# NSA layer of a two-block model in fp32: the compressed branch's projection columns first, its chain of steps between the row groups

## The chip, the cores and the metric

One core of a Trainium2 chip runs the whole program in one launch. The metric is the device time of one execution in microseconds (us), as the median of several runs. TensorE is PE in the rows (its weight loads are PEld), VectorE is DVE, ScalarE is ACT, GpSimd is POOL, and SyncE is SP; the SP queue issues the DMA transfers of the weights.

## The reference, cut to what matters

The program computes a first block of two layers, then a second block of two layers, each with a mixer, an output projection and a feed-forward net. The change lies in the mixer of the second block's first layer (NSA). There are 256 tokens, 12 query heads of 64 in 2 groups. With 256 tokens there are only 4 blocks of selectable keys and all are taken, so the selected and the window branch are both causal attention, each with its own keys and values.

```
proj = h @ w_in                       # q | six k/v slices of 128 | 36 gates | 256 memory queries
q = rope(q); k_slc = rope(k_slc); k_win = rope(k_win)
def compress_blocks(u, pos_emb, w1, b1, w2, b2):      # for k_cmp and for v_cmp
    blocks = u[:, idx] + pos_emb[:, None, :]          # 15 overlapping blocks of 32 tokens
    return gelu(flat(blocks) @ w1 + b1) @ w2 + b2     # 2048 -> 256 -> 64
kc = rope(compress_blocks(k_cmp, ...)); vc = compress_blocks(v_cmp, ...)
p_cmp = masked_softmax(q . kc * scale, cmp_end <= t)
gates = sigmoid(gate_logit + gate_b)
o = gates0 * (p_cmp @ vc) + gates1 * o_slc + gates2 * o_win
```

## The kernel before, in words

Every engine runs its own queue in the order in which the code writes it down. There is no scheduler: `nsa_pe`, `nsa_v`, `nsa_a` and `nsa_g` each write the queue of one engine for this stage, and they meet only in semaphores (`put` counts one up, `wait_ge(*got(...))` waits for the count that an event had).

**Weights.** All weights pass through one stream of items, numbered in the order in which PE takes them. An item is at most 1024 columns of 128 partitions. SP loads tiles of at most 2048 columns into three buffers (`raw`) and refills one as soon as the items of the tile three before have been split. ACT copies an item to its rounded part (`split_hi`, L368), DVE subtracts that from the original for the remainder (`split_lo`, L381), and PE multiplies with both, so that each product is made of three passes. There are six places for split items in this stage, so item n can be split only when PE is done with item n-6. ACT and DVE split ahead where the code says so: `split_hi(a, q, event)` splits all items up to the last of that event plus a lead (5 items, 4 for the items of the compression), whatever the item is needed for, and later instructions of the engine wait behind it.

**The NSA stage.** Three groups of rows are projected with tokens on the partitions (`group(0)` and `group(1)`: queries and keys, 4 items each of two chunks x 512 columns; `group(2)`: values and gates, 4 items of 584 columns), and six blocks of 128 columns with features on the partitions (the loop over `c0`, L422 to L427; c0 = 0 and 2 are the compressed keys and values, c0 = 4 the memory queries; an item each). The compression chain is:

- U: 16 small DVE adds (L2363) gather the blocks and add the position term; ACT rounds U (`Uh`, L2507), POOL makes the remainder (`Ul`, L2538);
- steps 0, 1 and 3, 4 (`compress_pe`): two items each of the first compression weight, for keys and for values; ACT copies each result (L2472);
- steps 2 and 5: transposes (L2296), the gelu on ACT (L2479, with a table load), DVE spreads it (`hrep`, L2403);
- step 6: the second weight (L2308, with a DVE add each, L2409); step 7: rope of the compressed keys, a transpose, and the operands `kcB` and `vcB` (L2416 to L2431);
- (b, 0), (b, 1), (b, 2) for both halves b of the tokens: scores (L2326), softmax (DVE L2441 to L2462, ACT L2523), transposes (L2332) and a copy (`cpt`, L2527).

Rope of queries and keys is eight long DVE operations (`rope_v`, L770 to L774). Then `turned_pe` transposes the result (L784) and ACT and DVE copy it out (L803, L798). The gates are an exp on ACT (L2514) and four small DVE operations.

**The attention** runs in rounds of units of two jobs: step 0 is the scores on PE (L619), 1 mask, maximum (DVE L668, L686) and exp (ACT L745), 2 the scaling with 1/sum and gate (DVE L690 to L698, ACT L726), 3 the transposes (PE L628) with copies (ACT L754, DVE L706), 4 the product with the values (PE L643, and the compressed branch's share L646), copied by ACT (L759) and DVE (L720). The list `chain` says which steps of the compression stand ahead of which round. Seven PSUM banks turn in a ring.

## Time and profile before

| what | us |
|---|---|
| median of 3 runs (1324.72 to 1330.0) | 1329.7 |
| profiled execution, its own time | 1329.96 |
| its span on the core | 1328.2 |
| PE busy in it | 1142.6 |
| DVE busy in it | 964.5 |
| ACT busy in it | 692.3 |

The span is what the profiler saw between the first and the last instruction; 1.8 us of the execution's time lie around it. Matmuls overlap, so a busy share of PE is not a share of its peak. The mean granted TensorE clock of the execution is 0.924 of full speed.

### The profile page before, as it was taken

Reading aid. Unit: us, or ns where it says so; the run is one execution under the profiler, and the core shown is the slowest. Engines: PE = TensorE matmul, PEld = TensorE weight load, DVE = VectorE, ACT = ScalarE, POOL = GpSimd, SP = SyncE. Lnnn points to the kernel's source line nnn. Section 1 sums busy time; section 2 is a strip of 40 time slices with the busy share of each in tenths; the row PEclk is TensorE's granted clock in tenths of the full one; section 3 lists DMA queues with packets and bytes.
Section 4 is the critical chain, followed back from the end, with each engine's and each line's share of the span. In section 5 each row is a group of like instructions: output and inputs, shape, how many; then the busy total and the mean of one; then the engine's idle time right before and its main releaser. Section 6 shows DMA issues by size and latency. Waiting matters only on the chain.

```text
span 1328.2 us, 24918 instructions
## 1 busy us (share of the span) xinstructions
PE 1142.6 (86%) x10403; PEld 1062.7 (80%) x10403; DVE 964.5 (73%) x1722; ACT 692.3 (52%) x1261; POOL 151.7 (11%) x113
## 2 busy tenths in 40 slices
PE   6799876979799758948976699999999959999997
PEld 6688765969678748848965599999999848999997
DVE  5787954666778855577768867888867576788873
ACT  5642256555532366555345845565655274565562
POOL 2000000110000001142000001223110000123210
PEclk9999986989899967978986989999999879999999
DMA  8332110344231103415530034554556403455461
GB/s 340 127 100 93 65 64 1 135 151 157 90 128 66 65 1 142 139 69 186 179 128 25 1 129 157 173 177 159 199 203 211 150 1 101 156 173 175 159 207 63
DMA packets 24736, 167.54 MB, mean 126 GB/s; under 512 B 2737, under 2 KB 2865, under 8 KB 8497
## 3 DMA queue, kind: packets, MB, share of 16 engines
q1 hardware_dynamic: 24624, 165.96, 35.8%
q8 instruction: 82, 1.34, 0.4%
q14 instruction: 30, 0.24, 0.1%
HBM read 164.90 MB, written 1.05 MB: 125 GB/s over the span
## 4 chain that ended last, share of the span: by engine, by line
PE 48%; DVE 29%; ACT 17%; issue 4%; DMA 2%; POOL 0%; DVEq 0%; SPq 0%; ACTq 0%; POOLq 0%
PE ps L427 9%; PE ps L422 9%; PE ps L424 9%; DVE WL L381 8%; ACT WH L368 3%; DVE FR L381 3%; PE ps L445 3%; PE ps L453 3%; PE ps L447 3%; ACT ARENA L745 2%; PE ps L643 2%; DMA raw<-wst_in 2%; ACT FR L368 1%; ACT ARENA L2136 1%; ACT L484 1%
## 5 line engine op out<-in xcount | busy, mean ns | idle before, releaser
L381 DVE TENSOR_TENSOR WL<-raw,WH 128x1024 fp32r<-128x1024 f32 (+4 forms) x225 | 274.0, 1240 | 104.6 <-ACT WH L368 104.0
L422 PE MATMUL ps<-FR,WH 128*128 128x256 f32 x1248 | 305.3, 285 | 21.8 <-ACT WH L368 16.5
L424 PE MATMUL ps<-FR,WH 128*128 128x256 f32 x1248 | 301.2, 282 | 1.3 <-DVE FR L493 0.8
L368 ACT ACTIVATE WH<-raw 128x1024 fp32r<-128x1024 f32 (+4 forms) x225 | 218.3, 988 | 101.8 <-PE ps L427 55.4
L422 PEld LDWEIGHTS ps<-FR,WH 128*128 128x128 f32 x1248 | 240.4, 193 | 26.9 <-ACT WH L368 13.6
L424 PEld LDWEIGHTS ps<-FR,WH 128*128 128x128 f32 x1248 | 240.0, 192 | 3.2 <-DVE FR L493 1.9
L422 PE MATMUL ps<-FR,FR 128*128 128x256 f32 x680 | 169.1, 286 | 2.9 <-ACT FR L368 2.2
L427 PE MATMUL ps<-FR,WL 128*128 128x256 f32 x1248 | 170.1, 279 | 0.5 <-DVE WL L381 0.5
L424 PE MATMUL ps<-FR,FR 128*128 128x256 f32 x680 | 167.9, 284 | 0.2 <-DVE FR L493 0.2
L427 PEld LDWEIGHTS ps<-FR,WL 128*128 128x128 f32 x1248 | 155.7, 189 | 0.7 <-DVE WL L381 0.7
L381 DVE TENSOR_TENSOR FR<-raw,FR 128x1024 fp32r<-128x1024 f32 (+2 forms) x100 | 127.3, 1297 | 34.5 <-ACT FR L368 34.5
L422 PEld LDWEIGHTS ps<-FR,FR 128*128 128x128 f32 x680 | 130.4, 192 | 5.4 <-ACT FR L368 3.6
L424 PEld LDWEIGHTS ps<-FR,FR 128*128 128x128 f32 x680 | 130.6, 192 | 0.6 <-DVE FR L493 0.4
L368 ACT ACTIVATE FR<-raw 128x1024 fp32r<-128x1024 f32 (+2 forms) x100 | 99.9, 1013 | 33.7 <-PE ps L427 18.7
L2136 ACT ACTIVATE ARENA<-ARENA,vec 128x256 f32<-128x256 f32 x88 | 48.2, 594 | 113.2 <-DVE ARENA L2087 113.2
L2181 POOL TENSOR_TENSOR ARENA<-ARENA 128x256 f32<-128x256 f32 x44 | 76.8, 1746 | 217.3 <-ACT ARENA L2148 217.3
L475 POOL TENSOR_TENSOR ARENA<-ARENA 128x512 f32<-128x512 f32 x32 | 45.4, 1419 | 465.7 <-DVE FR L493 152.1
L427 PE MATMUL ps<-FR,FR 128*128 128x256 f32 x680 | 95.7, 283 | 0.0
L445 PE MATMUL ps<-WH,FR 128*128 128x512 f32 (+4 forms) x200 | 79.6, 402 | 16.3 <-DVE ZR L1498 8.4
L427 PEld LDWEIGHTS ps<-FR,FR 128*128 128x128 f32 x680 | 87.7, 191 | 0.0
L643 PE MATMUL ps<-ARENA 128*64 128x128 f32 x400 | 36.5, 332 | 48.4 <-ACT ARENA L754 38.4
L2095 DVE SCALAR_TENSOR_TENSOR ARENA<-ARENA,vec 128x254 f32<-128x254 f32 (+1 forms) x176 | 76.6, 475 | 1.6
(320 smaller groups left out, 1825.9 us busy)
## 6 DMA issues: line engine op xcount, KB each, us to landing
raw<-wst_in SPq DMA_DIRECT2D x124, 1024.0 KB, 5.0
raw<-wst_in SPq DMA_DIRECT2D x14, 768.0 KB, 4.2
raw<-wst_in SPq DMA_DIRECT2D x11, 896.0 KB, 4.7
raw<-wst_in SPq DMA_DIRECT2D x4, 968.0 KB, 4.7
raw<-wst_in SPq DMA_DIRECT2D x2, 912.0 KB, 4.6
cst<-cst_in SPq DMA_DIRECT2D x1, 1681.0 KB, 15.3
X<-xT_in SPq DMA_DIRECT2D x2, 512.0 KB, 6.3
ARENA<-memT_in SPq DMA_DIRECT2D x1, 1024.0 KB, 4.8
```

Of the source, the lines that this page charges most:

```text
L368: a.activation(hi[:, 0:cols], src, ACT.Copy).then_inc(*put("split_hi", ("hi", i)))
L381: v.tensor_tensor(lo[:, 0:cols], src, hi[:, 0:cols].bitcast(F32), SUB).then_inc(*put("split_lo", ("lo", i)))
L422: pe.matmul(out, hv[:, k, :], src.hi[:, c, :], start=k0 == 0 and k == ks[0], stop=False)
L424: pe.matmul(out, hv[:, k, :], src.lo[:, c, :], start=False, stop=False)
L427: ins = pe.matmul(out, lv[:, k, :], src.hi[:, k0 + k, :], start=False, stop=k0 + n == kc and k == ks[-1])
L445: pe.matmul(outs[b], src.hi[:, c, t], hv[:, k, :], start=c == 0, stop=False)
L447: pe.matmul(outs[b], src.lo[:, c, t], hv[:, k, :], start=False, stop=False)
L475: g_.tensor_tensor(sq[0], sq[0], sq[n], ADD).then_inc(*put("square_sum", ("summed", tag, 2 * n)))
L643: ins = pe.matmul(ps[p, o:o + 128], x.v(i, kb), x.pt[:, t:t + 128], start=lead and kb == 0, stop=end and kb == nkb - 1)
L2095: v.scalar_tensor_tensor(u, p2[:, 256 * w:256 * w + 256 - d], vcol("conv_w_2", l, 44 * (2 - d) + c), u, MUL, ADD) \
L2136: a.activation(m.ub[2 * (i % 3) + w], m.pb[i % 3][:, 256 * w:256 * w + 256], ACT.Identity, bias=vcol("conv_b_2", l, c), scale=vcol("conv_w ...
L2181: g_.tensor_tensor(m.fb[n % 3], u[0], u[1], MUL).then_inc(*put("ffn_g", ("f", l, n)))
```

## The change

The queues of PE, DVE, ACT are written in another order, and the copy of the first compression product gets a buffer of its own (`hT`), so that it no longer waits for rope to be done with `TA`. The projection starts with the four blocks of columns of the compressed branch; the compression steps 0 and 1 stand between `group(1)` and `group(2)`, steps 3 and 4 behind `group(2)`; the memory queries come last, and steps 2 and 5 follow them, ahead of the transposes of the roped rows. On DVE rope moves behind steps 0 and 1. Steps 6 and 7 and the softmax of the compressed branch are put ahead of rounds 0 to 4, one entry each.

```
             self.STC = m.some(2, 24)
+            self.hT = m(512)
...
-            chain = [("compress", 2), ("compress", 5), ("compress", 6), ("compress", 7), (1, 0), (0, 0), (1, 1), (0, 1), (1, 2), (0, 2)]
-            self.steps = lambda engine: chain[0:3] + ordered(rounds[0], engine) + chain[3:5] + ordered(rounds[1], engine) + chain[5:7] + \
-                ordered(rounds[2], engine) + chain[7:] + [x for t in rounds[3:] for x in ordered(t, engine)]
+            chain = [[("compress", 6)], [("compress", 7)], [(1, 0), (0, 0)], [(1, 1), (0, 1)], [(1, 2), (0, 2)]]
+            self.steps = lambda engine: [x for n, t in enumerate(rounds) for x in (chain[n] if n < 5 else []) + ordered(t, engine)]
...
-        group(0)
-        group(1)
-        for c0 in range(0, 6, 2):
+        def cols(c0):
             ps = begin_bank("zc", c0)
             for i in range(2):
                 feat("a_w_in_2", 0, NSA_F[c0 + i], m.H, "HN", ps[:, 256 * i:256 * i + 256], "zc", c0)
+
+        cols(0)
+        cols(2)
+        group(0)
+        group(1)
+        compress_pe(0)
+        compress_pe(1)
         group(2)
-        for x in (0, 1, 3, 4):
-            compress_pe(x)
+        compress_pe(3)
+        compress_pe(4)
+        cols(4)
+        compress_pe(2)
+        compress_pe(5)
         turned_pe("N", m.zt, 8)
...
-        group(0)
-        group(1)
-        q.wait_ge(*got("zt na", 1))
-        q.wait_ge(*own("proj_v"))
-        rope_v(v, q, "N", m.zt, 16, 64, 32, "r64c", "r64s", m.TA, m.TB)
...
+        group(0)
+        group(1)
+        compress_v(v, q, 0)
+        compress_v(v, q, 1)
+        q.wait_ge(*got("zt na", 1))
+        q.wait_ge(*own("proj_v"))
+        rope_v(v, q, "N", m.zt, 16, 64, 32, "r64c", "r64s", m.TA, m.TB)
         group(2)
...
-            q.wait_ge(*got("rope", "N"))
             q.wait_ge(*got("hT", x))
-            a.activation(m.TA[0:30, 256 * x:256 * x + 256], ps[0:30, 0:256], ACT.Copy).then_inc(*put("cmp_a", ("hT a", x), free))
+            a.activation(m.hT[0:30, 256 * x:256 * x + 256], ps[0:30, 0:256], ACT.Copy).then_inc(*put("cmp_a", ("hT a", x), free))
```

ACT's and DVE's queues get the same order as PE's; the DVE adds of U stand right behind the splits for c0 = 2, and ACT's rounding of U behind its copy of c0 = 2.

The first place is DVE's queue from the end of its first splits to the first copy behind rope. FR and WL are places of split items (L381), 128x1024 and 128x584 the two sizes. Before:

```order
L2347 COPY ARENA<-ps 128x512
L381 TENSOR_TENSOR FR_50<-raw,FR_49 128x1024
L381 TENSOR_TENSOR FR_52<-raw,FR_51 128x1024
L381 TENSOR_TENSOR FR_54<-raw,FR_53 128x1024
L381 TENSOR_TENSOR WL<-raw,WH 128x1024
L2347 COPY ARENA<-ps 128x512
L770 TENSOR_TENSOR ARENA<-ARENA,cst 128x1024
```

And of the change, from the last splits ahead of rope to the copy of `group(2)`:

```order
L381 TENSOR_TENSOR WL<-raw,WH 128x584 x2
L770 TENSOR_TENSOR ARENA<-ARENA,cst 128x1024
...
L774 TENSOR_TENSOR ARENA<-ARENA 128x1024
L381 TENSOR_TENSOR WL<-raw,WH 128x1024
L381 TENSOR_TENSOR FR_50<-raw,FR_49 128x1024
L381 TENSOR_TENSOR FR_52<-raw,FR_51 128x1024
L381 TENSOR_TENSOR FR_54<-raw,FR_53 128x1024
L381 TENSOR_TENSOR WL<-raw,WH 128x1024
L2355 COPY ARENA<-ps 128x292
```

Rope stood behind the copy of `group(1)` with eight items split ahead of it; it now stands behind the splits of the items of `group(2)`, and five items of 1024 columns, the first four of them those of steps 3 and 4, are split only behind it.

The second place is ACT's queue from the last items ahead of the attention to its first exp (L745). Before:

```order
L368 ACTIVATE FR_53<-raw 128x1024
L2472 ACTIVATE ARENA<-ps 30x256
L803 ACTIVATE ARENA<-ps 128x512 x2
L2514 ACTIVATE ARENA<-ARENA 128x36 x2
L484 ACT_TABLE_LOAD
L2479 ACTIVATE ARENA<-ps,vec 128x30 x4
L484 ACT_TABLE_LOAD
```

And of the change:

```order
L2487 ACTIVATE ARENA<-ps 30x256
L368 ACTIVATE FR_51<-raw 128x1024
L368 ACTIVATE FR_53<-raw 128x1024
L368 ACTIVATE WH<-raw 128x1024
L2516 ACTIVATE ARENA<-ps 128x512
L484 ACT_TABLE_LOAD
L2494 ACTIVATE ARENA<-ps,vec 128x30 x4
L803 ACTIVATE ARENA<-ps 128x512 x2
L2537 ACT_TABLE_LOAD
L2537 ACTIVATE ARENA<-ARENA 128x36 x2
L484 ACT_TABLE_LOAD
```

The gelu (L2479, now L2494) moves ahead of the copies of the transposes and of the gates' exp, behind three more splits and the copy of the memory queries (L2516); there are three table loads where there were two.

The third place is PE's queue from the second compression weight (L2308, now L2316) to the first product with the values (L643). Before:

```order
L2308 MATMUL ps<-raw,ARENA 128x64 x8
L619 MATMUL ps<-ARENA 128x256 x4
L2314 MATMUL ps<-cst,ARENA 128x128
L2326 MATMUL ps<-ARENA 128x32 x6
L619 MATMUL ps<-ARENA 128x256 x4
L2326 MATMUL ps<-ARENA 128x32 x6
L619 MATMUL ps<-ARENA 128x256 x4
L2332 MATMUL ps<-cst,ARENA 128x128 x6
L628 MATMUL ps<-cst,ARENA 128x128 x8
L619 MATMUL ps<-ARENA 128x256 x4
L643 MATMUL ps<-ARENA 64x128 x8
```

And of the change:

```order
L2316 MATMUL ps<-raw,ARENA 128x64 x8
L619 MATMUL ps<-ARENA 128x256 x4
L2322 MATMUL ps<-cst,ARENA 128x128
L619 MATMUL ps<-ARENA 128x256 x4
L2334 MATMUL ps<-ARENA 128x32 x12
L619 MATMUL ps<-ARENA 128x256 x4
L628 MATMUL ps<-cst,ARENA 128x128 x8
L619 MATMUL ps<-ARENA 128x256 x4
L2340 MATMUL ps<-cst,ARENA 128x128 x6
L643 MATMUL ps<-ARENA 64x128 x8
```

The second unit's scores (L619) now stand ahead of the compressed scores (L2326, now L2334), which follow one another without scores between them, and the transposes of the compressed probabilities (L2332, now L2340) stand behind those of the first unit.

## Rows read from the trace of the kernel before

**Rows 1.** The page: busy time of each engine.

```profile
PE 1142.6 (86%) x10403; PEld 1062.7 (80%) x10403; DVE 964.5 (73%) x1722; ACT 692.3 (52%) x1261; POOL 151.7 (11%) x113
```

**Rows 2.** Stretches of the NSA stage: busy us by engine, granted clock, DMA share, GB/s.

```profile
619.80:643.60 23.80, 23.70 (x96) 19.25 (x97) 15.90 (x14) 12.92 (x15) 0.00 (x0) 0.93 0.67 239
643.60:660.40 16.80, 16.80 (x146) 16.76 (x145) 13.33 (x16) 6.36 (x9) 0.00 (x0) 1.00 0.38 140
668.90:680.00 11.10, 11.05 (x96) 10.20 (x97) 9.57 (x10) 6.40 (x9) 0.00 (x0) 1.00 0.59 195
680.00:688.80 8.80, 2.50 (x22) 2.11 (x20) 6.51 (x19) 5.78 (x13) 0.00 (x0) 0.83 0.16 67
688.80:705.00 16.20, 14.96 (x65) 12.50 (x65) 9.02 (x35) 3.22 (x10) 0.00 (x0) 0.50 0.36 130
725.00:755.00 30.00, 21.29 (x248) 17.08 (x248) 27.07 (x91) 23.19 (x92) 0.00 (x0) 1.00 0.01 1
```

**Rows 3.** PE in order of time: start, duration, what, idle time before it.

```profile
664.78 0.69 PE L453 MATMUL ps<-FR,FR 128*128 128x292 f32 x4
666.39 0.70 PE L453 MATMUL ps<-FR,FR 128*128 128x292 f32 x4
668.95 0.28 PE L2285 MATMUL ps<-WH,FR 128*30 128x256 f32 x1 [1.86 <-issue]
688.83 3.65 PE L2308 MATMUL ps<-raw,ARENA 128*128 128x64 f32 x16 [5.00 <-DVE ARENA L2403]
692.41 2.08 PE L619 MATMUL ps<-ARENA 64*128 64x256 f32 x8
696.10 2.77 PE L2326 MATMUL ps<-ARENA 128*128 128x32 f32 x12 [1.21 <-DVE ARENA L2431]
719.69 1.98 PE L643 MATMUL ps<-ARENA 128*64 128x128 f32 x16 [1.14 <-ACT ARENA L754]
734.74 1.09 PE L643 MATMUL ps<-ARENA 128*64 128x128 f32 x16 [1.89 <-ACT ARENA L754]
```

**Rows 4.** ACT in order of time, around the end of the projections.

```profile
682.15 1.06 ACT L368 ACTIVATE FR<-raw 128x1024 fp32r<-128x1024 f32 x1 [1.60 <-DMA raw<-wst_in]
685.80 0.35 ACT L2514 ACTIVATE ARENA<-ARENA 128x36 f32<-128x36 f32 x2 [1.38 <-DVE ARENA L2373]
686.17 1.28 ACT L484 ACT_TABLE_LOAD   x1
687.47 0.81 ACT L2479 ACTIVATE ARENA<-ps,vec 128x30 f32<-128x30 f32 x4
```

**Rows 5.** The chain that ended last: the transfer before that split.

```profile
677.25 4.88 DMA raw<-wst_in
```

**Rows 6.** DVE in order of time: rope, U, splits, and the steps behind `hrep`.

```profile
644.68 1.23 DVE L770 TENSOR_TENSOR ARENA<-ARENA,cst 128x1024 f32<-128x1024 f32 x1
650.86 1.22 DVE L774 TENSOR_TENSOR ARENA<-ARENA 128x1024 f32<-128x1024 f32 x1
660.23 5.28 DVE L2363 TENSOR_TENSOR ARENA<-ARENA,vec 64x120 f32<-64x120 f32 x16
670.99 2.35 DVE L381 TENSOR_TENSOR FR<-raw,FR 128x1024 fp32r<-128x1024 f32 x2
692.52 0.22 DVE L2409 TENSOR_TENSOR ARENA<-ps,vec 128x64 f32<-128x64 f32 x1 [0.63 <-PE ps L2308]
695.68 0.37 DVE L2431 COPY ARENA<-ps 64x16 f32<-64x16 f32 x2
712.06 0.36 DVE L2451 TENSOR_TENSOR ARENA<-ARENA,cst 128x192 f32<-128x192 f32 x1 [1.41 <-ACT ARENA L2523]
713.79 0.16 DVE L690 RECIPROCAL STAT<-STAT 128x2 f32<-128x2 f32 x1
715.11 0.68 DVE L668 SCALAR_TENSOR_TENSOR ARENA<-ps,cst 128x512 f32<-128x512 f32 x1
717.75 0.68 DVE L706 COPY ARENA<-ps 128x512 f32<-128x512 f32 x1
```

More of the change, by code:

```diff
@@ L2295, in compress_pe @@
                 for hc in range(2):
-                    ins = pe.transpose(ps[:, 32 * hc:32 * hc + 30], m.TA[0:30, 256 * v + 128 * hc:256 * v + 128 * hc + 128], ident[0:30, 0:30])
+                    ins = pe.transpose(ps[:, 32 * hc:32 * hc + 30], m.hT[0:30, 256 * v + 128 * hc:256 * v + 128 * hc + 128], ident[0:30, 0:30])
                 ins.then_inc(*put("cmp_pe", ("hid", v)))
@@ L2347, in group, with cols @@
             v.tensor_copy(dst, ps[:, 0:NSA_N[g]]).then_inc(*put("proj_v", ("zt n", g) if g < 2 else ("zv n", 1), free))
-        group(0)
-        group(1)
-        q.wait_ge(*got("zt na", 1))
-        q.wait_ge(*own("proj_v"))
-        rope_v(v, q, "N", m.zt, 16, 64, 32, "r64c", "r64s", m.TA, m.TB)
-        for c0 in range(0, 6, 2):
+        def cols(c0):
             split_lo(v, q, "zc", c0)
+        cols(0)
+        cols(2)
         for x in range(2):
@@ L2364, in nsa_v @@
                                         bc(vcol("pos", None, 16 * x + 8 * y, 8)[p, :], 2, 15), ADD).then_inc(*put("cmp_v", ("U",)))
-        group(2)
-        for x in (0, 1, 3, 4):
-            compress_v(v, q, x)
+        group(0)
[5 more added lines that the diff above has]
+        rope_v(v, q, "N", m.zt, 16, 64, 32, "r64c", "r64s", m.TA, m.TB)
+        group(2)
+        compress_v(v, q, 3)
+        compress_v(v, q, 4)
+        cols(4)
+        compress_v(v, q, 2)
+        compress_v(v, q, 5)
         turned_v(v, q, "N", m.FT, 8)
@@ L2495, in group, with cols @@
             a.activation(dst, ps[:, 0:NSA_N[g]], ACT.Copy).then_inc(*put("proj_a", ("zt na", g) if g < 2 else ("zv n", 0), free))
-        group(0)
-        group(1)
-        for c0 in range(0, 6, 2):
+        def cols(c0):
             split_hi(a, q, "zc", c0)
@@ L2504, in nsa_a @@
                 .then_inc(*put("proj_a", ("zc a", c0) if c0 < 4 else ("qm",), free))
+        cols(0)
+        cols(2)
         q.wait_ge(*got("U"))
@@ L2507, in nsa_a @@
         a.activation(fl(m.Uh), fl(m.U), ACT.Copy).then_inc(*put("cmp_a", ("Uh",)))
+        group(0)
+        group(1)
+        compress_a(a, q, 0)
+        compress_a(a, q, 1)
         group(2)
-        for x in (0, 1, 3, 4):
-            compress_a(a, q, x)
+        compress_a(a, q, 3)
+        compress_a(a, q, 4)
+        cols(4)
+        compress_a(a, q, 2)
+        compress_a(a, q, 5)
         turned_a(a, q, "N", m.FT, 8)
```

## The prediction

> **What bounds the kernel now.** I read the page first. PE is busy for 86% of the span [rows 1]: a change that only permutes PE's work can win no more than what PE waits in the stage. So the next view was the table of stretches of the NSA stage [rows 2]. Read its first number in each pair, the busy time of PE, against the length of the stretch. From 619.8 to 660.4 PE has no gap, from 668.9 to 680.0 none either. From 680.0 to 688.8 it works 2.5 of 8.8 us, and from there to 705.0 it is busy but its clock is 0.50: the lower of its two levels, 1.2 GHz.
>
> PE's own timeline says where the gaps lie [rows 3]. It waits 1.86 us at 668.95 (for the chain U, `Uh`, `Ul`) and 5.00 us at 688.83 (for `hrep`, behind the gelu). The first attention scores start at 692.41, the compressed ones at 696.10, the first product with the values at 719.69. That last moment is my anchor, because from there the rounds follow each other as before, and the output projection and what comes behind follow them.
>
> Who makes PE wait at 688.83 is read backwards in ACT's timeline [rows 4] and in the chain [rows 5]: a transfer of 4.88 us ends at 682.15, ACT splits that item, copies, loads a table at 686.17 and computes the gelu at 687.47. That item belongs to the output projection; ACT merely has it ahead of the gelu in its queue. DVE is the other engine to watch: rope is 7.40 us in one piece (644.68 to 652.08), U 5.28 us [rows 6].
>
> **What the change does, part by part.**
>
> *The PE stream.* It is the same work. By the stretches, the eight items of `group(0)` and `group(1)` take 23.8 us with a mean clock of 0.93; 7% of 23.8 is 1.7 us lost to the low clock at the start, which stays at the start whatever runs there, so the items themselves are 22.1. Six blocks of columns take 16.8, 2.80 each. The eight items of the compression take 11.1, 1.39 each. An item of `group(2)` takes 1.61 (664.78 to 666.39), four 6.4 [rows 2, 3]. New order from 619.8: four blocks and the 1.7 until 632.7; two groups until 654.8; four compression items until 660.4; `group(2)` until 666.8; four more until 672.4; the memory queries until 678.0. Before, the stream ended at 680.0. The difference is the wait for U: DVE can make U from 632.7 on, done by 638, rounded and split by about 642, and PE asks for it at 654.8. Gain 2.0.
>
> *Is PE fed?* U stands 5.28 us in DVE's queue, ACT waits behind it, and both split late; but nine items are split by then (lead 5 behind the fourth), and the tenth is wanted only at 632.7 + 5 x 2.76 = 646.5. Covered by some 5 us. Rope is the risky one. Ahead of it stands the split of item 19, which needs the place of item 13; PE leaves that at 654.8 + 2 x 1.39 = 657.6. A rounded part and a remainder of 584 columns are less than the 1.06 [rows 4] and 1.2 (2.35 for two [rows 6]) of 1024, together about 1.5: 659.1. Rope ends at 666.5. Item 20, the first of step 3, gets its remainder at 667.7. PE begins it at 666.8 and needs the remainder for its last third, at 667.7. It just fits; a stall of up to 0.5 is in the range. Then DVE makes one remainder in 1.18, PE uses one in 1.39: no further stall.
>
> *The gelu.* hT of the values is copied without waiting for rope, early enough. But ACT still has to split ahead: items 25, 27, 28, 29, 30 stand before the copy of the memory queries and the gelu. Items 29 and 30 are in a tile that SP requests when item 24 has its remainder: 666.5 + 5 x 1.18 = 672.4. It lands 4.88 later [rows 5], 677.3. Two splits of ACT, 2.0: 679.3. The copy of the memory queries, at most the 0.68 that DVE's of that size takes [rows 6]: 680.0. Table load 1.28, gelu 0.81 [rows 4]: 682.1. From the gelu's end (688.28) to PE's start (688.83) were 0.55, so PE starts the second weight at 682.7, 6.1 earlier. The gelu is not hidden: behind the stream PE has only its transposes, the 2.5 of work in the stretch from 680.0 [rows 2], until 680.5; it waits some 2 us.
>
> *The gates and the third table load.* Gelu ahead of the gates' exp means one more load, 1.28 [rows 4]. It waits for nothing, so it runs right behind ACT's two copies (at most 0.68 each, as above): 683.5 to 684.8. The exps take 0.35 [rows 4]: 685.1. DVE's four small operations, at the 0.22 of one of 64 columns [rows 6] and a little for each wait, about 1.0: 686.1. DVE has the adds of step 6 behind them; the last add needs PE's last product at 682.7 + 3.65 = 686.4 [rows 3]. Cover 0.3, price 0.
>
> The Trainium skill (ScalarE: Activation LUTs, section "What ACT_TABLE_LOAD costs") puts a switch of sets at 1.28 for the load plus 1.38 for a drain. In this trace the gelu starts 1.30 after the load does, so the row decides. By the page the gates would come about 1.4 later, 1.1 of it uncovered, and the forecast would be 1324.5.
>
> *Steps 6 and 7.* From 688.83 to `kcB` (695.68 + 0.37) took 7.22 [rows 3, 6]; the same operations now: 689.9. PE's first scores run at 686.4, the second unit's at about 689.0, both 2.08, so the compressed scores start at 691.0, take 2 x 2.77, and end at 696.5.
>
> *DVE up to the anchor.* Behind 696.5: the second half's softmax up to its exp, at most the 1.73 of its rest (712.06 to 713.79): 698.2. Unit 0's scaling 1.32 (713.79 to 715.11), unit 1's masks and maxima 2.64 (715.11 to 717.75): 702.2 [rows 6]. ACT's exps come in order, so DVE waits the same 1.41 as at 712.06: 703.6. Then both halves' rests, 2 x 1.73, and 1.32 + 2.64: 711.0. Before, that point was 717.75. So -6.75. The copies `cpt` now stand on ACT between this round's copy and PE's first product with the values; the first, 384 columns, costs about 0.4 there (under the 0.68 of 512), where it was hidden; but my 698.2 is a ceiling, some 0.3 above what is likely. Net -6.65 at the anchor.
>
> *Behind it.* Same rounds, same items. One item more is split ahead of the output projection; PE has three ready there anyway, so nothing. Sum: 1329.96 - 6.6 = 1323.4. The execution with the profile lies 0.3 above the median of the runs shown (1329.7), so the ratio is 0.995, at the bound of what such a measurement tells from no change (0.5%, 6.6 us).
>
> **The rivals.**
>
> 1. *The clock rises early.* The scores now run almost without a gap from 686.4 to 691.0. If PE gets its 2.4 GHz back there, the compressed scores shrink from 5.5 to about 3.0, and DVE starts 2.5 earlier behind them. For it: a product form that took 1.98 at 719.69 took 1.09 at 734.74 [rows 3]. Against it: PE was busy for 15.0 of 16.2 us from 688.8 to 705.0 and its clock stayed at 0.50 throughout [rows 2]. 1323.4 - 2.5 = 1320.9. The Trainium skill (TensorE: Matmul & The Clock Gate, section "What's actually happening") has the clock come back with sustained activity; this stretch shows activity of this kind without it.
>
> 2. *The chain is late after all.* The gelu hangs on rope's end, five remainders, a transfer, two splits. If the transfer takes 2 us longer, because three tiles are requested within 5 us, or DVE gets to rope 2 us later (PE then stalls too), all behind is late by that much: the gain is 6.6 - 2 to 6.6 - 4. For it: SP's refills hang on DVE alone there. Against it: the mean DMA share of the stretch was only 0.59 [rows 2]. 1325.4 to 1327.4, 1326.4 in the middle.
>
> 3. *The change does nothing*, because the attention's start is set by DVE, whose work is the same. For it: DVE is the next engine [rows 1]. Against it: at 688.83 and 696.10 PE waits, and DVE waits for PE. 1329.9.
>
> 4. *Slower: the low clock stays.* The clock has to rise while the rounds run. From 725.0 to 755.0 it was 1.00 with PE busy for 21.3 of 30.0 [rows 2]. PE's work between 704 and 713 is now thin (scores and transposes are done earlier), so the rise can come later, or not in this stage. At 1.98 instead of 1.09 the 21.3 become 38.7 [rows 3]: 8.7 more than the 30.0, if PE then is alone on the path. 1329.96 - 6.6 + 8.7 = 1332.1. It decides from the point where more than three quarters of those 30 us are at the low clock; a rise one round late costs about 1 and lies within the forecast. Against it: the rounds themselves are as dense as before.
>
> **How the numbers follow.** The forecast 0.52, its own range 1321.9 to 1325.2 (a stall of 0.5 at rope, a late clock of 1; the ceilings not reached on the other side). Rival 1 0.15, rival 2 0.24, rival 3 0.05, rival 4 0.04. The range leaves out rivals 3 and 4, takes in rival 1 with some 2 us below it for the spread of the runs shown, and rival 2 up to its end: 1318.5 to 1327.8. Faster by over 0.5% means under 1323.1: some 0.4 of the forecast's share (its middle lies 0.3 above that bound), 0.21, rival 1 with nearly all, 0.14, and 0.05 for a median drawn low as one of the runs shown: 0.40. Slower by over 0.5%, above 1336.3: only an extreme of rival 4, 0.03. Within: 0.57.
>
> **What would show each step.** Right: PE without a gap from its first item to 678; U's first add at 632.7; rope from about 659 to 666.6; a wait of about 2 us, not 5, before the second weight, which starts near 682.7; the gates' reciprocals done before the last add of step 6; compressed scores at 691.0; the first product with the values at 713. Wrong: a gap before the remainder of item 20, a transfer landing after 678, DVE waiting for the gates' exp, or a clock of 0.50 behind 722.

## The result, and the profile after

The changed kernel takes 1319.23 us (median of 5 runs, 1317.24 to 1321.39), the kernel before 1329.5 (5 runs, 1324.72 to 1330.0). The ratio is 0.9921, 95% interval [0.9906, 0.9936]. Forecast was 1323.4, range 1318.5 to 1327.8: inside the range, and 4.2 us faster than the forecast. Timed a second time (c3_after_timed below) the ratio was 0.9944 [0.9925, 0.9963], 1321.28 us. The profiled execution took 1319.23 us, its span is 1317.2.

Its stage begins at 618.80 us. In the kernel before it began at 619.89; two rows of PE there, its first matmul and the second half's compressed scores:

```profile
619.89 0.47 PE L445 MATMUL ps<-WH,FR 128*128 128x512 f32 x1 [2.27 <-ACT WH L368]
700.81 2.77 PE L2326 MATMUL ps<-ARENA 128*128 128x32 f32 x12
```

The identical program ahead of the stage was 1.09 us faster in this execution, so whoever compares a moment of it with the forecast adds 1.09 first. The stretches that answer to [rows 2], each moved by that or by the later gain:

```profile
618.80:642.60 23.80, 23.80 (x144) 21.79 (x145) 19.41 (x28) 14.13 (x17) 2.29 (x1) 0.93 0.50 180
667.80:678.90 11.10, 11.10 (x100) 10.63 (x99) 7.83 (x8) 4.34 (x6) 0.00 (x0) 1.00 0.69 248
678.90:687.70 8.80, 4.68 (x31) 3.51 (x29) 7.14 (x30) 7.47 (x14) 0.00 (x0) 0.84 0.19 43
688.00:700.00 12.00, 11.36 (x49) 9.21 (x49) 9.51 (x30) 3.35 (x11) 0.00 (x0) 0.50 0.57 221
717.40:747.40 30.00, 21.27 (x248) 17.07 (x248) 27.08 (x91) 23.18 (x92) 0.00 (x0) 1.00 0.01 1
```

PE's queue has no gap until its transposes end; the stretch in which it waits still lies behind them, but is shorter. The rounds (last row) are what they were within two hundredths: 21.27 busy of 30.0 against 21.29 [rows 2].

PE in order of time, the rows that answer to [rows 3]:

```profile
618.80 0.35 PE L422 MATMUL ps<-FR,WH 128*128 128x256 f32 x1 [2.12 <-issue]
677.64 1.97 PE L784 MATMUL ps<-cst,ARENA 128*128 128x128 f32 x16
683.01 1.97 PE L2316 MATMUL ps<-raw,ARENA 128*128 128x64 f32 x16 [3.40 <-DVE ARENA L2419]
687.95 0.48 PE L2322 MATMUL ps<-cst,ARENA 128*128 128x128 f32 x1 [0.97 <-DVE ARENA L2437]
690.37 5.33 PE L2334 MATMUL ps<-ARENA 128*128 128x32 f32 x24
712.08 1.98 PE L643 MATMUL ps<-ARENA 128*64 128x128 f32 x16 [3.21 <-ACT ARENA L2550]
717.38 1.09 PE L643 MATMUL ps<-ARENA 128*64 128x128 f32 x16 [0.23 <-ACT ARENA L754]
```

The wait for U (1.86 at 668.95) is gone. The wait before the second weight is 3.40 instead of 5.00. The anchor, the first product with the values, is at 712.08: 93.28 us behind the stage's first matmul, where it was 719.69 - 619.89 = 99.80. The stage gained 6.52 us; forecast were 6.65.

ACT around the gelu (answers to [rows 4]) and the chain of work that ended last there (answers to [rows 5]):

```profile
677.89 1.06 ACT L368 ACTIVATE FR<-raw 128x1024 fp32r<-128x1024 f32 x1 [0.55 <-DMA raw<-wst_in]
682.38 1.10 ACT L803 ACTIVATE ARENA<-ps 128x512 f32<-128x512 f32 x2
683.50 1.28 ACT L2537 ACT_TABLE_LOAD   x1
684.79 0.35 ACT L2537 ACTIVATE ARENA<-ARENA 128x36 f32<-128x36 f32 x2
```

```profile
665.83 1.22 DVE WL L381
667.05 3.41 DVE FR L381 x3
670.46 1.15 DVE WL L381
671.67 6.20 DMA raw<-wst_in
677.89 1.06 ACT FR L368
678.95 0.95 ACT WH L368
679.90 0.48 ACT ARENA L2516
680.40 1.28 ACT L484
681.69 0.81 ACT ARENA L2494 x4
```

This is the path that the forecast named: rope, five remainders, the request, the transfer, two splits, the copy, the table, the gelu. One link is off: the transfer took 6.20 us, not 4.88. And the chain goes on over a link that the forecast had beside it: the copies of the transposes, the third table load at 683.50, the gates' exp.

DVE behind it (answers to [rows 6]):

```profile
658.39 1.22 DVE L770 TENSOR_TENSOR ARENA<-ARENA,cst 128x1024 f32<-128x1024 f32 x1
685.05 0.18 DVE L2393 TENSOR_SCALAR ARENA<-ARENA 128x36 f32<-128x36 f32 x1 [0.74 <-ACT ARENA L2537]
685.72 0.38 DVE L2395 RECIPROCAL ARENA<-ARENA 128x36 f32<-128x36 f32 x1
686.01 0.55 DVE L2425 TENSOR_TENSOR ARENA<-ps,vec 128x64 f32<-128x64 f32 x4
689.50 0.38 DVE L2447 COPY ARENA<-ps 64x16 f32<-64x16 f32 x2
709.87 0.68 DVE L706 COPY ARENA<-ps 128x512 f32<-128x512 f32 x1
```

All four adds of step 6 (L2425) run in one row behind the gates' reciprocals, while in [rows 6] the last one waited for PE: now DVE's own queue was late, and DVE itself waited 0.74 us for the gates' exp.

**Where the time went.** Every profiled span here splits into three pieces: up to the stage's first matmul (identical code in all kernels), from there to the first L643, and from there to the end (the same work; only how many of the output projection's items are split before it differs). Starts of rows on PE and the spans give:

| execution | ahead | stage | behind | span |
|---|---|---|---|---|
| before | 619.89 | 99.80 | 608.5 | 1328.2 |
| before again (c1) | 620.10 | 99.81 | 608.4 | 1328.3 |
| changed | 618.80 | 93.28 | 605.1 | 1317.2 |
| changed again (c2) | 617.09 | 94.17 | 607.4 | 1318.7 |
| changed, third (c3) | 621.45 | 92.90 | 609.3 | 1323.6 |
| s1_columns_first | 621.67 | 97.22 | 607.7 | 1326.6 |
| s2_old_rounds | 617.88 | 94.24 | 611.4 | 1323.5 |
| s3_new_rounds | 617.85 | 96.48 | 608.9 | 1323.2 |
| g1_gates_later | 622.31 | 92.85 | 609.2 | 1324.4 |
| i3_no_lead | 619.44 | 90.68 | 617.4 | 1327.5 |
| i6_no_lead_tail | 622.19 | 89.70 | 609.4 | 1321.3 |
| i4_all_hidden | 619.75 | 86.29 | 616.1 | 1322.1 |
| i5_splits_in_tail | 619.35 | 86.28 | 609.4 | 1315.0 |

Of the 11.0 us between the first two profiled spans, 1.1 are ahead of the stage, 6.5 in it, 3.4 behind it. The experiments had to say which of these the change makes. In the tables and texts below, "stage" means the stretch from the stage's first matmul to the anchor, and "forecast" what was expected before that run.

### The profile page after: what moved, and what is told of

Read it like the earlier page. It is cut to its first block, busy times and chain, and to the rows that moved or that the text cites. A ratio compares the mean times of both kernels' runs of the same rounds, so it can differ in the third digit from the quotient of the medians.

```text
span 1317.2 us, 24918 instructions
## 1 busy us (share of the span) xinstructions
PE 1134.6 (86%) x10403; PEld 1055.9 (80%) x10403; DVE 964.3 (73%) x1722; ACT 693.7 (53%) x1262; POOL 151.7 (12%) x113
## 3 DMA queue, kind: packets, MB, share of 16 engines
q8 instruction: 82, 1.34, 0.4%
## 4 chain that ended last, share of the span: by engine, by line
PE 49%; DVE 28%; ACT 17%; issue 4%; DMA 2%; POOL 0%; DVEq 0%; SPq 0%; ACTq 0%; POOLq 0%
PE ps L427 10%; PE ps L422 10%; PE ps L424 9%; DVE WL L381 7%; ACT WH L368 3%; PE ps L445 3%; DVE FR L381 3%; PE ps L453 3%; PE ps L447 3%; ACT ARENA L745 2%; DMA raw<-wst_in 2%; PE ps L643 2%; ACT L484 1%; ACT FR L368 1%; ACT ARENA L2136 1%
## 5 line engine op out<-in xcount | busy, mean ns | idle before, releaser
L381 DVE TENSOR_TENSOR WL<-raw,WH 128x1024 fp32r<-128x1024 f32 (+3 forms) x225 | 272.9, 1234 | 103.1 <-ACT WH L368 102.8
L422 PE MATMUL ps<-FR,WH 128*128 128x256 f32 x1264 | 310.6, 286 | 23.6 <-ACT WH L368 16.1
L424 PE MATMUL ps<-FR,WH 128*128 128x256 f32 x1264 | 306.5, 283 | 1.3 <-DVE FR L493 0.8
L368 ACT ACTIVATE WH<-raw 128x1024 fp32r<-128x1024 f32 (+3 forms) x225 | 218.3, 987 | 105.1 <-PE ps L427 54.1
L422 PEld LDWEIGHTS ps<-FR,WH 128*128 128x128 f32 x1264 | 243.9, 193 | 28.9 <-ACT WH L368 13.6
L424 PEld LDWEIGHTS ps<-FR,WH 128*128 128x128 f32 x1264 | 243.7, 193 | 3.2 <-DVE FR L493 1.9
L427 PE MATMUL ps<-FR,WL 128*128 128x256 f32 x1264 | 173.9, 280 | 0.3 <-DVE WL L381 0.3
L422 PE MATMUL ps<-FR,FR 128*128 128x256 f32 x664 | 165.1, 286 | 2.3 <-ACT FR L368 2.2
L424 PE MATMUL ps<-FR,FR 128*128 128x256 f32 x664 | 163.8, 284 | 0.2 <-DVE FR L493 0.2
L427 PEld LDWEIGHTS ps<-FR,WL 128*128 128x128 f32 x1264 | 159.5, 191 | 0.6 <-DVE WL L381 0.6
L381 DVE TENSOR_TENSOR FR<-raw,FR 128x1024 fp32r<-128x1024 f32 (+2 forms) x100 | 128.9, 1314 | 30.5 <-ACT FR L368 30.5
L422 PEld LDWEIGHTS ps<-FR,FR 128*128 128x128 f32 x664 | 127.4, 192 | 4.5 <-ACT FR L368 3.6
L424 PEld LDWEIGHTS ps<-FR,FR 128*128 128x128 f32 x664 | 127.4, 192 | 0.6 <-DVE FR L493 0.4
L427 PE MATMUL ps<-FR,FR 128*128 128x256 f32 x664 | 93.2, 282 | 0.0
L427 PEld LDWEIGHTS ps<-FR,FR 128*128 128x128 f32 x664 | 85.3, 190 | 0.0
L643 PE MATMUL ps<-ARENA 128*64 128x128 f32 x400 | 35.3, 324 | 51.6 <-ACT ARENA L754 37.4
```

The lines of the kernel that those rows point to most:

```text
L368: a.activation(hi[:, 0:cols], src, ACT.Copy).then_inc(*put("split_hi", ("hi", i)))
L381: v.tensor_tensor(lo[:, 0:cols], src, hi[:, 0:cols].bitcast(F32), SUB).then_inc(*put("split_lo", ("lo", i)))
L422: pe.matmul(out, hv[:, k, :], src.hi[:, c, :], start=k0 == 0 and k == ks[0], stop=False)
L424: pe.matmul(out, hv[:, k, :], src.lo[:, c, :], start=False, stop=False)
L427: ins = pe.matmul(out, lv[:, k, :], src.hi[:, k0 + k, :], start=False, stop=k0 + n == kc and k == ks[-1])
L643: ins = pe.matmul(ps[p, o:o + 128], x.v(i, kb), x.pt[:, t:t + 128], start=lead and kb == 0, stop=end and kb == nkb - 1)
```

## The experiments

The kernel before was timed beside each group: 1330.28 us for the first four and for the next four, 1329.08 for the last three.

**Three parts alone.** s1_columns_first is the kernel before with one edit, for all three engines:

```
-        group(0)
-        group(1)
-        for c0 in range(0, 6, 2):
+        cols(0)
+        cols(2)
...
+        group(0)
+        group(1)
+        cols(4)
         group(2)
```

with U behind the second block, and rope behind U. The compression's steps and the rounds stand as before.

> The kernel before, with only the four blocks of columns of the compressed branch and U put first; steps 0, 1, 3, 4 and all behind them stand where they stood. My theory (the gain of the change is a sum of three parts, 2.0 us from the wait for U, about 4 from the chain from the end of the stream to the second weight, about 0.6 from the order of the rounds): PE waits no longer for U, everything behind moves 2.0 us, the first product with the values comes 97.8 us behind the first matmul of the stage (before 99.8), median 1.5 to 2.5 us under the kernel before. Rival (the wait for U was hidden, since DVE's and ACT's chain to the gelu is what ends last): 99.8 us and no gain.

Measured: 1326.07 us (12 runs), ratio 0.9972 [0.996, 0.9984]; stage 97.22, forecast 97.8. By the ratio that is 3.7 us under before (forecast 1.5 to 2.5). Moving the columns is worth 2.6 us in the stage: the wait for U is gone and the first transposes behind the stream (L784) come 2.02 us earlier, the 2.0 of the forecast; the other 0.57 is gained at the second pair of transposes of steps 2 and 5, which waited 1.34 us for ACT's copy before and waits 0.77 here. The 5.00 us wait isn't touched:

```profile
688.02 3.65 PE L2312 MATMUL ps<-raw,ARENA 128*128 128x64 f32 x16 [5.00 <-DVE ARENA L2408]
```

s2_old_rounds is the changed kernel with the steps among the rounds as they were:

```
-            chain = [[("compress", 6)], [("compress", 7)], [(1, 0), (0, 0)], [(1, 1), (0, 1)], [(1, 2), (0, 2)]]
+            chain = [("compress", 6), ("compress", 7), (1, 0), (0, 0), (1, 1), (0, 1), (1, 2), (0, 2)]
+            self.steps = lambda engine: chain[0:1] + ordered(rounds[0], engine) + chain[1:3] + ...
```

> The changed kernel, with steps 6 and 7 and the compressed softmax spread over the rounds as before. My theory: the rounds' order is the small part: 94.0 us from the first matmul of the stage to the first product with the values (the changed kernel has 93.3), median about 0.7 us above the changed kernel. Rival (most of what the change gained beyond the forecast comes from the rounds): 3 us or more above the changed kernel.

Measured: 1324.42 us (6 runs), 0.995 [0.9933, 0.9968]; stage 94.24, forecast 94.0. s2 contains s1's edit, so what lies between them, the early steps 0 and 1, the buffer `hT` and the early gelu, is worth 97.22 - 94.24 = 3.0 us of the stage (expected were about 4). The median decides nothing: by the ratios s2 is 3.9 us slower than the changed kernel's first timing and 0.8 slower than its second, and the interval overlaps both.

s3_new_rounds is the kernel before with only the new order of steps 6, 7 and the softmax:

```
+            chain = [[("compress", 2), ("compress", 5), ("compress", 6)], [("compress", 7)], [(1, 0), (0, 0)], [(1, 1), (0, 1)], [(1, 2), (0, 2)]]
+            self.steps = lambda engine: [x for n, t in enumerate(rounds) for x in (chain[n] if n < 5 else []) + ordered(t, engine)]
```

> The kernel before, with only the order of steps and rounds of the change (steps 2, 5, 6 ahead of round 0, step 7 ahead of round 1, both halves' scores together ahead of round 2). My theory: 99.1 us from the first matmul of the stage to the first product with the values (before 99.8), median about 0.7 us under the kernel before. Rival: 3 us or more under it.

Measured: 1327.87 us (12 runs), 0.9983 [0.9973, 0.9992]; stage 96.48, forecast 99.1. A miss: the order of the rounds alone was worth 3.3 us of the stage, not 0.7, and by the ratio 2.3 us of the median, between the forecast and the rival. PE shows where:

```profile
686.83 3.65 PE L2307 MATMUL ps<-raw,ARENA 128*128 128x64 f32 x16 [5.00 <-DVE ARENA L2402]
694.42 2.87 PE L2325 MATMUL ps<-ARENA 128*128 128x32 f32 x24
714.33 1.97 PE L643 MATMUL ps<-ARENA 128*64 128x128 f32 x16 [3.21 <-ACT ARENA L2526]
```

And the stretch with the compressed scores, the granted clock in the last column but two:

```profile
694.00:697.00 3.00, 3.00 (x29) 2.67 (x26) 2.90 (x7) 1.25 (x5) 0.00 (x0) 1.00 1.02 431
```

Both halves of the compressed scores are one row of 24 here, 2.87 us at the higher clock, where the kernel before needed two rows of 12 at 696.10 [rows 3] and 700.81, 2.77 each at the lower one. In this execution the clock had risen when they came (1.00 from 694 to 697, 0.50 ahead of it). In the changed kernel the same row took 5.33 in all three profiles. By these two rows 5.33 - 2.87 = 2.5 of the 3.3 are the clock's, an estimate, and the 0.9 that is left is near the 0.7 of the forecast: the order was sized right, the clock wasn't foreseen. On top of the early chain the order is worth 94.24 less 93.28, 94.17 or 92.90, which is 0.1 to 1.3; there the low clock lies on the compressed scores.

**The price of the gates.** g1_gates_later takes DVE's four operations for the gates out of step 6's way:

```
-        for b in range(2):
-            g = m.gates[:, b, :]
...
             if x == "compress":
                 compress_v(v, q, s)
+                for b in range(2 if s == 7 else 0):
+                    g = m.gates[:, b, :]
```

> The changed kernel, with DVE's four small operations of the gates moved from ahead of step 6 to behind step 7. In the changed kernel PE's second weight ran at 2.4 GHz and ended about 685.0, DVE's last add of step 6 at 686.6, because it stood behind the gates' exp. If that order cost something (my reading of the trace after; the prediction put it at nothing): the compressed scores start 1.0 us earlier and the median falls by about 1 us against the changed kernel. Rival (the prediction's own term, price nothing, since PE's product ends last): no difference.

Measured: 1324.26 us (6 runs), 0.9942 [0.9921, 0.9964]; stage 92.85 against 93.28, 94.17 and 92.90. The end of `kcB` comes 70.36 us behind the stage's first matmul (changed kernel: 71.08, 71.69, 70.72), so step 6 does gain 0.4 to 1.3. At the anchor the difference is 0.05 to 1.3, no more than the three profiles of the changed kernel differ among themselves, and the forecast of 1 us in the median isn't borne out: by the ratios g1 lies 2.8 us above the changed kernel's first timing and 0.3 under its second. Whether a rest of the gain reaches the anchor stays open; the four operations then stand ahead of the masks and maxima in the same queue.

**The same kernels again.** c1_before_again and c2_after_again are the two kernels unchanged, one execution each.

> The kernel before once more, unchanged, for a second trace. The changed kernel's trace was 10.7 us shorter, of which only 6.5 lie between the first matmul of the stage and the first product with the values; 1.1 lie ahead of the stage and 3.4 behind the anchor, in stretches with a lower granted clock. If those 4.5 us are the spread of the clock from one execution to the next: this trace differs from the first one of the same kernel by something like 1 us in the same places (ahead of the stage, at the end of the attention, at the start of the last mixer), with the stretch from first matmul to anchor within 0.3 of 99.8. If they belong to the change: this trace repeats the first one in all of them.

> The changed kernel once more, unchanged, for a second trace. Same question: first matmul of the stage to anchor within 0.3 of 93.3 by either theory; the places outside it repeat if they belong to the change, and differ by about 1 us each if they are the clock's spread.

> The changed kernel once more, unchanged, timed beside the other two. If the 10.3 us of its first timing are the change's, it stands at 1318.5 to 1321 us, 9 to 11 us under before. If part of them is where the low clock happened to fall in those runs, it stands at 1321 to 1324, and its gain behind the stage is not the same as in the first profile.

Measured: 1330.43, 1320.82, and for c3 1321.28 us (6 runs, 1317.27 to 1326.06), ratio 0.9944 [0.9925, 0.9963]. The second execution of before repeats the first in all three columns of the table within 0.3 us, though not in the clock ahead of the stage: 1.00 from 20 to 60 us in the first, 0.91 in the second. The three of the changed kernel agree on the stage within 1.3 us (92.9 to 94.2; c2's 94.17 is 0.9 from the 93.3 expected, and its second weight took 3.65 us, not 1.97). They differ by 4.4 ahead of it and by 4.2 behind it, where the code is the same. c3's 1321.28 lies in the range expected if the first timing owed part of its 10.3 us to the clock. Two places where the clock differs, from 20 to 60 us and at the end of the last attention, first in the changed kernel's first profile:

```profile
20.00:60.00 40.00, 35.03 (x279) 33.37 (x278) 28.39 (x48) 25.49 (x42) 3.51 (x3) 1.00 0.51 185
1084.00:1094.00 10.00, 7.83 (x60) 6.59 (x59) 3.85 (x7) 2.04 (x7) 0.00 (x0) 0.66 0.01 2
```

and in its third:

```profile
20.00:60.00 40.00, 36.21 (x264) 34.66 (x264) 26.56 (x47) 23.36 (x38) 4.24 (x3) 0.87 0.45 167
1090.00:1100.00 10.00, 8.25 (x52) 6.84 (x51) 3.98 (x7) 0.99 (x3) 0.00 (x0) 0.50 0.01 2
```

The granted clock is 1.00 against 0.87, 0.66 against 0.50. These are not the only places: the third profile is 1.0 us behind the first in the same DVE operation at 71 us, and 2.65 at the stage. Another is the attention itself: from the anchor to the end of the last product with the values it takes 52.7, 55.7 and 53.8 us in the three profiles (before 53.8 twice). So the same code gives and takes up to 4 us on either side of the stage.

A small part of the 3.4 us behind it does belong to the change. The kernel before has four items left to split on DVE between the last attention product and the first addition to X, the changed kernel three, since one more was split ahead. The addition comes 6.69 us behind the product in both profiles of before and 5.92 to 5.94 in all three of the changed kernel; at the fourth addition 0.5 us of that is left. s1 and s3, with four splits, have 6.7 as well. (s2 has three and still 6.69: its last product ran at the lower clock, and the addition waits 0.50 us for PE.)

**Two ways to shorten the gelu's path.** i3_no_lead is the changed kernel without the splits of items 28 to 30 ahead of the gelu (on ACT and DVE, both made later, where the output projection asks for them):

```
-            split_hi(a, q, "zc", c0)
+            split_hi(a, q, "zc", c0, ahead=2 if c0 == 4 else None)
```

> The changed kernel, without the three items (28, 29, 30) that ACT and DVE split ahead between the memory queries and the gelu. My theory (the gelu waits for a transfer and two splits that only the output projection needs): the gelu starts as soon as PE has the memory queries and the transposes, the second weight starts 2.0 to 2.6 us earlier, median 1.5 to 2.5 us under the changed kernel. Rival (the output projection then pays the splits back): the stretch to the anchor shrinks, the output projection starts with waits on PE, no gain in the median.

Measured: 1328.09 us (12 runs), 0.9982 [0.9968, 0.9996]: by the ratios 5 to 8 us slower than the changed kernel, where 1.5 to 2.5 faster was the forecast. The theory of the gelu held: the second weight starts 61.6 us behind the stage's first matmul, 2.6 earlier, and the stage is the shorter one (90.68, 9.1 under before). The rival came true beside it: 8.9 us more lie behind the stage than in the kernel before.

i4_all_hidden does that, and leaves PE something to do while ACT computes the gelu: the memory queries come behind step 5.

```
         compress_pe(4)
-        cols(4)
+        turned_pe("N", m.zt, 8)
         compress_pe(2)
         compress_pe(5)
-        turned_pe("N", m.zt, 8)
+        cols(4)
```

Step 4 also splits only two items ahead, DVE's remainder of the last item comes behind the gates, and ACT loads the table for the gates and computes their exps ahead of the copy of the memory queries.

> The changed kernel, with the transposes of the roped rows and steps 2 and 5 put ahead of the memory queries on PE and ACT, the memory queries' 5.6 us thus covering the gelu and the gates, no third table load, and no splits ahead of the gelu beyond those that PE needs. My theory: PE runs without a wait from the first item to the second weight, which starts at 61.0 us behind the first matmul of the stage instead of 64.2, and since the gates are long done the compressed scores start about 4 us earlier; median 3.5 to 4.5 us under the changed kernel. Rival (DVE's queue, not PE's wait, sets the compressed scores): gain 1 us or less.

Measured: 1323.73 us (6 runs), 0.9951 [0.9933, 0.997]: by the ratios 1 to 4 us above the changed kernel, where 3.5 to 4.5 under it was the forecast. The stage is 86.29, 7.0 us shorter than in the changed kernel (13.5 under before), with no wait before the second weight; but 7.6 us more lie behind it than in the kernel before. DVE in the changed kernel, from its splits to the first addition to X (L1961):

```profile
766.94 2.36 DVE L381 TENSOR_TENSOR WL<-raw,WH 128x1024 fp32r<-128x1024 f32 x2 [1.20 <-ACT WH L368]
769.22 1.22 DVE L381 TENSOR_TENSOR FR<-raw,FR 128x1024 fp32r<-128x1024 f32 x1
770.73 0.69 DVE L1961 TENSOR_TENSOR X<-X,ps 128x512 f32<-128x512 f32 x1 [0.30 <-PE ps L427]
```

And DVE, ACT and PE of i4 in the output projection:

```profile
756.76 0.42 DVE L720 TENSOR_TENSOR FR<-ps,FR 128x256 fp32r<-128x256 f32 x1 [2.64 <-ACT FR L759]
762.00 2.36 DVE L381 TENSOR_TENSOR FR<-raw,FR 128x1024 fp32r<-128x1024 f32 x2 [1.20 <-ACT FR L368]
764.27 3.50 DVE L381 TENSOR_TENSOR WL<-raw,WH 128x1024 fp32r<-128x1024 f32 x3
768.31 1.07 ACT L368 ACTIVATE FR<-raw 128x1024 fp32r<-128x1024 f32 x1 [2.62 <-DMA raw<-wst_in]
769.41 1.23 DVE L381 TENSOR_TENSOR FR<-raw,FR 128x1024 fp32r<-128x1024 f32 x1 [1.64 <-ACT FR L368]
770.55 0.68 DVE L1961 TENSOR_TENSOR X<-X,ps 128x512 f32<-128x512 f32 x1
788.52 0.58 PE L422 MATMUL ps<-FR,FR 128*128 128x256 f32 x1 [4.26 <-ACT FR L489]
```

Read them in order: DVE idles for 2.64 us in the tail of the attention; then six splits stand in its queue ahead of the first addition to X, three more than in the changed kernel; since they free the loading places late, the next tile is late too, by 2.62 us; the addition (770.55) comes 10.7 us behind the end of the last attention product (759.85), against 5.9 in the changed kernel (770.73 behind 764.80); the later additions follow it at 5.4 to 5.7 us each, and PE, done with the projection, waits 4.26 us for the normalised rows. Nothing of this is visible in the stretch up to the anchor.

**The splits in the attention's tail.** i5_splits_in_tail is i4 and i6_no_lead_tail is i3 with one addition: on ACT items 28 to 30 are split ahead of its last copy but one, on DVE ahead of its last two output subtractions.

```
+        tail = [n for n, (x, s) in enumerate(m.steps("V")) if s == 4 and x not in ("compress", 0, 1) and x.mate]
+        for n, (x, s) in enumerate(m.steps("V")):
+            if n in tail[-2:]:
+                split_lo(v, q, "zc", 4, ahead=4 if n == tail[-2] else None)
```

> This is the kernel of i4_all_hidden with one thing moved: ScalarE's splits of weight items 28 to 30 stand ahead of its copy of the last attention output but one (where it idled 4.42 us in i4), VectorE's ahead of its last two output subtractions (2.64 and 1.76 us idle). Theory: in i4 the stage was 13.6 us shorter than before at the first round's product, and 6.6 us of that were paid back in the output projection, because these three splits stood there ahead of its first addition to X (770.55 us, 10.8 us behind the end of the last attention product; 6.0 us in the changed kernel) and because the tiles behind them were loaded later (a wait of 2.62 us for a transfer at 768.31). Then nothing is paid back: first addition to X 6 us behind the last product, TensorE's idle stretch of 4.26 us at the first matmul on the normalised rows gone (under 0.3 us), 13.6 us under before, about 1316.7 us by a before of 1330.3, range 1314 to 1319. Rival: the output projection is bound by something else that a shorter stage meets sooner (the rate of the weight stream, the pace of VectorE and ScalarE of 5.66 us for two columns of X), and the time stays at 1322 to 1325.

> The changed kernel with the splits of items 28 to 30 taken from between the memory queries and the gelu to the end of the attention, as in i5. Theory: i3_no_lead gained 8.6 us in the stage (6.7 in the changed kernel) and paid 8.5 back behind it, all for want of these splits. With them in idle time of the tail the stage's gain is kept: 1330.3 - 8.6 = 1321.7 us, range 1319.5 to 1323.5, no idle stretch of 4.26 us on TensorE in the output projection. Rival: the lead itself isn't the cause, and it stays at 1326 to 1329.

Measured: i5 1316.61 us (5 runs, 1314.21 to 1317.68), 0.9898 [0.9885, 0.9912], in the expected range; i6 1317.91 us (6 runs), 0.9928 [0.9907, 0.9948], 1.6 us below its range. Part of i6's surplus is its stage, 10.1 us under before where i3's was 9.1: its compressed scores took 4.59 us, not 5.33. In both, 609.4 us lie behind the stage, against 616.1 and 617.4 without the addition. i5's tail:

```profile
753.41 2.35 DVE L381 TENSOR_TENSOR FR<-raw,FR 128x1024 fp32r<-128x1024 f32 x2
756.13 0.42 DVE L720 TENSOR_TENSOR FR<-ps,FR 128x256 fp32r<-128x256 f32 x1 [0.37 <-ACT FR L759]
758.10 1.22 DVE L381 TENSOR_TENSOR WL<-raw,WH 128x1024 fp32r<-128x1024 f32 x1
765.35 0.69 DVE L1961 TENSOR_TENSOR X<-X,ps 128x512 f32<-128x512 f32 x1 [0.28 <-PE ps L427]
784.25 0.38 PE L424 MATMUL ps<-FR,FR 128*128 128x256 f32 x1 [0.21 <-DVE FR L493]
```

The three splits fill idle time (DVE's wait for ACT's copy shrinks from 2.64 to 0.37), the first addition to X waits for PE alone, 5.9 us behind the last product, and PE's idle 4.26 is gone. i5 is the fastest version: 12.5 us under before, 4.7 under the changed kernel timed beside it, and the two intervals don't meet. i6's interval overlaps the changed kernel's. The theory of the lead is shown twice, by pairs that differ in these splits alone and whose intervals don't meet: i3 against i6, and i4 against i5.

## Why the prediction was right

**The stream.** Right. No gap; U begins at 631.38, which is 632.5 with the 1.09 added (forecast 632.7); rope 658.39 (659.5; forecast 659.1); item 20's remainder in time.

**The gelu.** The mechanism was right, the transfer was mis-sized. "It lands 4.88 later" failed: this one took 6.20 (6.67 in c2, 6.00 in c3), so the small form of rival 2 came true. It was the third of three tiles requested within 4.5 us (667.13, 669.40, 671.67), and they took 3.96, 5.65 and 6.20 in this order; before, the requests lay 6.1 us apart in all and the third took the 4.88. The sharing is argued from these times; no run sets the spacing alone. The splits end 1.7 us late, the second weight starts 64.2 us behind the stage's first matmul instead of 62.8 (64.5 and 63.8 in c2 and c3).

**The second weight.** The sum took its 3.65 us of the lower clock. In two of three profiles it ran at the higher one, 1.97 us, behind waits of 3.40 and 3.17 us; in c2 it took 3.65 behind a wait of 3.88, as before behind 5.00, and in g1 2.25 behind 3.87. The shorter waits go with the higher clock; that they cause it is argued. In the two profiles this gave PE back what the transfer had cost.

**The gates.** "Cover 0.3, price 0" failed where it was put: with PE at the higher clock its products were ready before the gates were, and `kcB` ends at 689.88, which is 71.1 us behind the first matmul (forecast 70.0). In c2, with the second weight at the lower clock, it held: the last add waits 0.26 us for PE. At the anchor the first profile is within 0.2 of the forecast all the same; g1 puts the price there between 0.05 and 0.4 us against the two profiles with the higher clock, too little to tell from 0. The 1.38 that the Trainium skill (ScalarE: Activation LUTs, section "What ACT_TABLE_LOAD costs") adds for a drain doesn't show: the copies end at 683.48, the load starts at 683.50, the first exp at 684.79, 1.29 later.

**DVE up to the anchor.** Right: 709.87 + 1.09 = 710.96, forecast 711.0. The anchor 93.15 behind the first matmul by forecast, 93.28, 94.17 and 92.90 measured.

**How much of that is luck.** The path is the one named, but two of the prediction's own signs of being wrong appeared in the first profile: a transfer that lands after 678 (677.87 + 1.09 = 679.0) and DVE waiting for the gates' exp. The transfer was too cheap by 1.1 to 1.8 us and the gates' price was left out; against them stands a second weight that was too dear by 1.7 in two of three profiles. That the sum came out within 0.3 in these two, and 1.0 off in c2, where the second weight cost what the forecast said, is a cancelling of errors.

**Rival 1** didn't come about: the compressed scores took 5.33 us in all three profiles of the changed kernel. Its price is real, though. In s3 the clock did rise early, as shown above. In i4 PE has the memory queries until the second weight, and its clock stays up:

```profile
680.00:685.00 5.00, 4.33 (x37) 3.56 (x36) 4.53 (x19) 1.00 (x2) 0.00 (x0) 1.00 0.34 93
685.00:690.00 5.00, 4.47 (x36) 3.55 (x32) 4.74 (x15) 2.19 (x8) 0.00 (x0) 0.92 0.28 116
```

and the same row of 24 takes 2.87 us: the 2.5 that rival 1 put on it. **Rival 3** is out: the stage gained 6.5. **Rival 4** is out as the decider: in the first profile the clock is 1.00 from 717.4 to 747.4. In c2, though, it was back at 0.50 from 727.7 to 731.0, a third sign on the prediction's list. The "three quarters" from which this rival was to decide don't follow from its numbers either: 21.3 us reach 30.0 with half of PE's work at the lower clock (21.3 + 0.5 x 17.4).

**"Nothing behind it"** was nearly right. "PE has three ready there anyway, so nothing" was wrong by 0.8 us at the first addition to X and 0.5 at the fourth: the item split ahead took a split out of DVE's queue, and there DVE, not PE, ended last. The median lies 4.2 us under the forecast; in the profiled execution 1.1 are ahead of the stage and 3.4 behind it, where the code is the same. The medians of the two timings are 10.3 and 7.8 us under before, the stage's gain in the three profiles 6.5, 5.6 and 6.9. The split explains 0.5 of what lies between them. Whether the rest, up to some 3 us, is chance or an indirect effect of the shorter stage on the clock stays open: c3's profile argues for chance (0.7 us more behind the stage than before has), but three profiles can't settle it.

## What to carry to other kernels

Work that an engine does ahead is not free to drop: before taking a lead out of a critical queue, look for the engine's idle rows between there and the moment it is needed, and put it into these. In i3 the stage ended 9.1 us earlier than before and 8.9 us came back, in i4 13.5 and 7.6, both in the output projection some 90 us later, where the splits left out had to be made up. And compare a gain from anchor to anchor inside the stage that was changed: the whole span carries some 4 us ahead and behind that belong to no edit.

## What the runs showed of the hardware

The granted clock of identical code differs between executions of one kernel: 0.87 against 1.00 from 20 to 60 us, and the start of the stage lies anywhere from 617.1 to 622.3 us in 13 profiles. The second weight (16 matmuls of 64 columns) takes 1.97 us where the clock is at its higher level and 3.65 at the lower one, in executions of one kernel. The Trainium skill (TensorE: Matmul & The Clock Gate, section "What's actually happening") has the watch over PE's activity run on its own time, not the kernel's, so that one kernel can come out differently from run to run; these profiles agree.

By the same section of the Trainium skill activity brings the clock back; from 688 to 700 us of the changed kernel PE was busy for 11.36 of 12.0 and the clock stayed at 0.50, its lower level of 1.2 GHz. In c2 PE had no gap at all from 682 to 696:

```profile
682.00:696.00 14.00, 14.00 (x62) 11.79 (x64) 10.16 (x42) 5.13 (x13) 0.00 (x0) 0.50 0.58 226
```

In s3 the same kind of work, without a gap from 686.83 on, had the clock back at 694. In i4 and i5, where projections run up to the second weight, it was 1.00 until 685 and 0.92 or 0.90 to 690. That the projections are the reason is argued, not shown.

The transfer of the tile ahead of the gelu took 4.88 us in the kernel before and 6.00 to 6.67 in the changed one; in its first profile the mean DMA share of the stretch was 0.69, before 0.59.
